# Feed-forward norms of two layers: rows are turned raw, the weight is multiplied in by feature columns, the root at the up evictions

## The reference, cut

```python
for layer in range(DEPTH):                       # DEPTH = 2
    h = rms_norm(x, g_mix[layer])
    qkv = h @ w_in[layer]
    ...
    x = x + mix @ w_out[layer]
    h2 = rms_norm(x, g_ffn[layer])               # the norm that the change touches
    x = x + conv_gated_mlp(h2, w_up[layer], conv_w[layer], conv_b[layer], w_down[layer])

def conv_gated_mlp(h, w_up, conv_w, conv_b, w_down):
    u = h @ w_up                                 # 1024 -> 2 x 2816
    u = causal convolution of width 3 along the tokens, per feature, + conv_b
    gate, val = jnp.split(u, 2, axis=-1)
    return (jax.nn.silu(gate) * val) @ w_down
```

## Time and profile before

| | |
|---|---|
| median of 3 runs | 1744.21 us |
| lowest, highest | 1742.28, 1744.73 us |
| the profiled execution, its own time | 1744.4 us |
| its span, first to last instruction | 1742.6 us |
| TensorE, VectorE, ScalarE, GpSimd busy | 97%, 66%, 47%, 41% of the span |
| mean granted TensorE clock | 0.996 |

### The profile page before, as it was taken

The page is one execution under the profiler, slowest core; times in us unless marked ns, Lnnn a source line. Parts: engine busy times, 40 slices in busy tenths (PEclk is TensorE's granted clock), DMA queues, the critical chain, the costliest instruction groups (busy, mean ns, idle before and its releaser), DMA issues.

```text
span 1742.6 us, 27224 instructions
## 1 busy us (share of the span) xinstructions
PE 1693.9 (97%) x10714; PEld 1456.7 (84%) x10714; DVE 1151.4 (66%) x2422; ACT 821.4 (47%) x1453; POOL 706.1 (41%) x384
## 2 busy tenths in 40 slices
PE   7999999999999998999999999999999999999997
PEld 6779998777799986544579999999999988888885
DVE  6755785756467585655332999999999644444443
ACT  5555655355476642122343554544444455555553
POOL 2424676133266811421163999700000144444443
PEclk9999999999999999999999999999999999999998
DMA  7333545463165463323353656544444466666664
GB/s 289 117 109 135 191 170 183 148 217 117 61 211 201 170 199 122 107 86 120 97 202 114 225 165 203 179 144 141 144 145 140 162 193 194 194 193 194 194 193 134
DMA packets 77456, 283.20 MB, mean 163 GB/s; under 512 B 8721, under 2 KB 8977, under 8 KB 77073
## 3 DMA queue, kind: packets, MB, share of 16 engines
q1 hardware_dynamic: 76032, 276.50, 48.5%
q10 hardware_dynamic: 1296, 4.97, 0.8%
HBM read 279.33 MB, written 2.10 MB: 161 GB/s over the span
## 4 chain that ended last, share of the span: by engine, by line
PE 79%; DVE 7%; POOL 4%; ACT 4%; issue 3%; DMA 1%; POOLq 0%; DVEq 0%; ACTq 0%
PE bank L542 63%; PE bank L533 8%; PE bank L597 5%; POOL wl L2117 4%; ACT wh L1112 2%; DVE att L1478 2%; PE bank L665 1%; DVE wl L1461 1%; ACT att L1115 1%; PE bank L967 1%; PE bank L889 1%; DVE ssb L1467 1%; DVE mix L1506 1%; DVE xs L1467 1%; PE bank L837 0%
## 5 line engine op out<-in xcount | busy, mean ns | idle before, releaser
L2117 POOL TENSOR_TENSOR wl<-raw,wh 128x1024 fp32r<-128x1024 f32 x213 | 547.6, 2582 | 696.5 <-ACT wh L1112 688.1
L542 PE MATMUL bank<-hh,wh 128*128 128x256 f32 x1856 | 526.5, 284 | 5.1 <-POOL wl L2117 4.2
L1112 ACT ACTIVATE wh<-raw 128x1024 fp32r<-128x1024 f32 x476 | 492.9, 1050 | 58.2 <-PE bank L542 39.4
L542 PE MATMUL bank<-hl,wh 128*128 128x256 f32 x1856 | 519.3, 280 | 0.0
L542 PE MATMUL bank<-hh,wl 128*128 128x256 f32 x1856 | 517.9, 279 | 0.0
L1461 DVE TENSOR_TENSOR wl<-raw,wh 128x1024 fp32r<-128x1024 f32 x263 | 353.8, 1351 | 93.8 <-ACT wh L1112 93.3
L542 PEld LDWEIGHTS bank<-hh,wh 128*128 128x128 f32 x1856 | 349.1, 188 | 6.6 <-POOL wl L2117 5.5
L542 PEld LDWEIGHTS bank<-hl,wh 128*128 128x128 f32 x1856 | 349.2, 188 | 0.0
L542 PEld LDWEIGHTS bank<-hh,wl 128*128 128x128 f32 x1856 | 349.0, 188 | 0.0
L1467 DVE TENSOR_TENSOR acl<-H,ach 128x256 fp32r<-128x256 f32 x128 | 87.6, 685 | 181.5 <-ACT ach L1115 181.5
L542 PE MATMUL bank<-wh,ach 128*128 128x512 f32 x512 | 199.2, 389 | 0.4 <-DVE acl L1467 0.4
(11 more groups left out here) (216 smaller groups left out, 2322.5 us busy)
## 6 DMA issues: line engine op xcount, KB each, us to landing
raw<-in_ut_dram SPq DMA_DIRECT2D x128, 512.0 KB, 3.5
raw<-in_vt_dram SPq DMA_DIRECT2D x128, 512.0 KB, 3.7
raw<-in_wup_dram SPq DMA_DIRECT2D x88, 512.0 KB, 4.1
raw<-in_win_dram SPq DMA_DIRECT2D x48, 512.0 KB, 4.6
raw<-in_wdown_dram SPq DMA_DIRECT2D x44, 512.0 KB, 4.2
raw<-in_wout_dram SPq DMA_DIRECT2D x24, 512.0 KB, 3.6
raw<-in_wga_dram SPq DMA_DIRECT2D x16, 512.0 KB, 3.6
raw<-in_wpq_dram SPq DMA_DIRECT2D x16, 512.0 KB, 4.7
```

Source lines behind the costliest of these rows:

```text
L542: m = p.e.matmul(out, lhs[i][a], rhs[i][b], start=start and i == 0 and j == 0, stop=stop and i == n - 1 and j == 2)
L1112: a.e.activation(high_of(u), raw_of(u), ACTF.Copy).then_inc(act_hi.up(("hi", u)), 1)
L2117: g.e.tensor_tensor(low_of(u), raw_of(u), high_of(u).bitcast(F32), ALU.subtract).then_inc(pool_lo.up(("lo", u)), 1)
```

## The change

The two feed-forward norms of the first block are taken apart.

- TensorE turns x itself, block by block, as soon as VectorE has added it (`x_turned`). The first block is turned ahead of the last quarter of the projection, and the dummy transposes of this place are gone.
- The weight is multiplied in when the turned blocks are split: ScalarE makes the high half of each block of 128 features with the feature's weight as its scale (`x_high`), and VectorE the low half with a multiply and a subtraction in one instruction (`x_low`). The weights come as 32 columns `gcol`, loaded once on ScalarE's queue. The two row units are no longer in `plan`, and no row is loaded or scaled.
- The root is found behind the splitting. VectorE spreads it to 128 columns per tile (`root_rows`), TensorE turns it after `f` = 0 of the up stage, and VectorE copies it out (`root_cols`). In each `f` VectorE then multiplies the bank of 128 x 512 in place by the root of each token, and the evictions wait for that (`upR`).
- In ScalarE's, VectorE's and GpSimd's lists, the splitting of the units of this place is moved against the norm's steps.
- Tensors move in SBUF: `hh` and `hl` are 2304 wide and the `f` stages start 16 elements in, `sta`, `con` and `sml` have other widths, and a scratch area is set to 1024.

```diff
-        hh, hl = scoped(sc_h, "hh", 2048, F32R), scoped(sc_h, "hl", 2048, F32R)
+        hh, hl = scoped(sc_h, "hh", 2304, F32R), scoped(sc_h, "hl", 2304, F32R)
...
-            stage(("row", "f", L), [(rows_d[2 + L], 1024, False)])
...
+        def hT_of(st):
+            o = 16 if st[0] == "f" else 0
+            return [w[:, o:o + 2048].rearrange("p (k t) -> p k t", k=8) for w in (hh, hl)]
...
+            def x_turned(st, t, k0, b, *after):
+                claim(b)
+                p.wait_ge(*after)
+                n = block_of(st, t, k0)[1]
+                for k in range(k0, k0 + n):
+                    m = p.e.transpose(banks[b][:, (k - k0) * 128:(k - k0) * 128 + 128], x[:, t, k * 128:(k + 1) * 128], ids[:, :])
...
@@ pe @@
-                for t in range(2):
-                    for j in (6, 7):
-                        out_unit(j, (t, ))
-                kept_streaming(8, 0)
-                for t, n in ((0, 22), (1, 6)):
-                    turned(("f", L), mix, 8, (t, ), lambda t, q: (dve_out, ("nrm", ("f", L), t, q)), of=(2, 3, 4, 5, 7))
-                    kept_streaming(n, 0)
+                st = ("f", L)
+                out_unit(6, (0, ))
+                out_unit(7, (0, ))
+                out_unit(6, (1, ))
+                free = ((0, 2, 3, 4, 7, 1), (0, 2, 5, 7, 6, 1))[L]
+                x_turned(st, 0, 0, free[0], dve_out, ("xa", L, 0, 0))
+                out_unit(7, (1, ))
+                x_turned(st, 1, 0, free[1], dve_out, ("xa", L, 1, 0))
+                x_turned(st, 1, 2, free[2], dve_out, ("xa", L, 1, 0))
+                x_turned(st, 0, 4, free[3], dve_out, ("xa", L, 0, 1))
+                x_turned(st, 1, 4, free[4], dve_out, ("xa", L, 1, 1))
+                x_turned(st, 1, 6, free[5], dve_out, ("xa", L, 1, 1))
                 for f in range(NTILE):
+                    if f == 1:
+                        p.wait_ge(dve_out, ("rb", st))
+                        for t in range(2):
+                            m = p.e.transpose(banks[b][:, tcols(t)], root_rows[:, tcols(t)], ids[:, :])
...
@@ act @@
+            def x_high(st, t, ks):
+                for k in ks:
+                    a.wait_ge(pe_out, ("T", st, t, block_of(st, t, k)[0]))
+                    do(hT_of(st)[0][:, k, tcols(t)], turned_block(st, t, k), ACTF.Identity, ("hTh", st, t, k), scale=gcol(st, k))
...
+                stream(first["wout", L] + 6)
+                x_high(st, 0, range(4))
                 half_squares(st, 0, mix, 0, dve_out, ev + (0, 0))
+                x_high(st, 1, range(4))
+                x_high(st, 0, range(4, 8))
+                x_high(st, 1, range(4, 8))
                 half_squares(st, 0, mix, 1, dve_out, ev + (0, 1))
-                stream(first["wout", L] + 6)
                 half_squares(st, 1, mix, 0, dve_out, ev + (1, 0))
                 half_squares(st, 1, mix, 1, dve_out, ev + (1, 1))
-                turned(st, (0,), 2)
                 stream(first["wout", L] + 7)
-                stream(first["row", "f", L])
-                turned(st, (1,), 2)
...
-                        a.wait_ge(pe_out, ("up", L, f, 1))
+                        a.wait_ge(dve_out, ("upR", L, f))
...
@@ dve @@
                 added(0, 0)
                 added(0, 1)
+                added(1, 0)
+                x_low(st, 0, range(4))
+                added(1, 1)
+                x_low(st, 1, range(4))
+                for k in range(4, 8):
+                    for t in range(2):
+                        x_low(st, t, (k, ))
                 stream(first["wout", L] + 6)
+                stream(first["wout", L] + 7)
                 mean(st, 0)
-                added(1, 0)
-                scale(st, 0, mix, row)
-                added(1, 1)
                 mean(st, 1)
-                turned(st, (0,), 1)
-                scale(st, 1, mix, row)
-                turned(st, (0,), 2, 1)
-                turned(st, (1,), 2)
-                stream(first["wout", L] + 7)
-                stream(row)
+                v.wait_ge(pool_out, ("rs", st, 0), ("rs", st, 1))
+                copy(root_rows.rearrange("p (a n) -> p a n", a=2), rstd[:, 0:2].unsqueeze(2).broadcast_to([128, 2, 128]), ("rb", st))
                 for f in range(NTILE):
                     stream(first["wup", L] + 2 * f)
                     stream(first["wup", L] + 2 * f + 1)
+                    if f == 0:
+                        v.wait_ge(pe_out, ("RT", st))
+                        copy(root_cols, ps("RT", st)[:, 0:256], ("R", st))
+                    both = ps("up", L, f)[:, :].rearrange("p (h t) -> p h t", h=2)
+                    v.wait_ge(pe_out, ("up", L, f, 1))
+                    tt(both, both, root_cols.unsqueeze(1).broadcast_to([128, 2, 256]), ALU.mult, ("upR", L, f))
...
@@ pool @@
+                stream(first["wout", L] + 6)
                 for t in range(2):
                     root(("f", L), t)
-                    g.wait_ge(dve_out, ("nrm", ("f", L), t, 1))
-                stream(first["wout", L] + 6)
                 stream(first["wout", L] + 7)
-                stream(first["row", "f", L])
...
-    nc = _bacc.Bacc("TRN2", target_bir_lowering=False, num_devices=1)
+    nc = _bacc.Bacc("TRN2", target_bir_lowering=False, num_devices=1, dynamic_dma_scratch_size=1024)
```

More of the change, by code:

```diff
@@ L114, in program @@
         early = ExitStack()
-        con_s = scoped(early, "con", K_W - 128)
-        sml_s = scoped(early, "sml", S_W)
+        con_s = scoped(early, "con", 1664)
+        sml_s = scoped(early, "sml", 896)
         tab_s = scoped(early, "tab", 8192)
@@ L303, in sml, with gcol, blocks, block_of @@
             return sml_s[:, c:c + n]
-        def hT(k, cols):
-            return hTh[:, k, cols], hTl[:, k, cols]
+        def hT_of(st):
+            o = 16 if st[0] == "f" else 0
+            return [w[:, o:o + 2048].rearrange("p (k t) -> p k t", k=8) for w in (hh, hl)]
+        def gcol(st, k):
+            return gcol_s[:, 8 * (st[1] + 2 * (st[0] == "f")) + k:8 * (st[1] + 2 * (st[0] == "f")) + k + 1]
+        def blocks(st, t):
+            return ((0, 2), (2, 2), (4, 2), (6, 2)) if st[0] == "f" and t else ((0, 4), (4, 4))
+        def block_of(st, t, k):
+            return [(k0, n) for k0, n in blocks(st, t) if k0 <= k < k0 + n][0]
+        def turned_block(st, t, k):
+            k0 = block_of(st, t, k)[0]
+            return ps("T", st, t, k0)[:, (k - k0) * 128:(k - k0) * 128 + 128]
+        def hT(st, k, cols):
+            return [w[:, k, cols] for w in hT_of(st)]
         iota = con(K_IOTA, 128)
@@ L334, in program @@
         tb = headtmp[:, 256:512].rearrange("p (h d) -> p h d", h=4)
+        root_rows, root_cols = headtmp[:, 0:256], headtmp[:, 256:512]
         NB = 4
@@ L590, in by_tokens @@
                         if plan[i][2]:
-                            m = mm3(banks[b][:, 0:cw], [hT(off + h * kper + k, tcols(t)) for k in range(kper)],
+                            m = mm3(banks[b][:, 0:cw], [hT(("n",), off + h * kper + k, tcols(t)) for k in range(kper)],
                                     [unit_pair(i, k, kper, slice(0, cw)) for k in range(kper)], h == 0, h == nu - 1,
@@ L616, in by_features @@
                             m = mm3(banks[b][:, 0:256], [unit_pair(i, k, kt, tcols(c)) for k in range(kt)],
-                                    [hT(off + k, ALLC) for k in range(kt)], True, True, ready)
+                                    [hT(("f", 2), off + k, ALLC) for k in range(kt)], True, True, ready)
                         else:
@@ L743, in out_unit @@
                             claim(b)
-                        m = mm3(banks[b][:, :], [hT(2 * h + k, tcols(t)) for k in range(2)], [unit_pair(i, k, 2, slice(0, 512)) for k in range(2)], h == 0, h == 3,
+                        m = mm3(banks[b][:, :], [hT(("n",), 2 * h + k, tcols(t)) for k in range(2)], [unit_pair(i, k, 2, slice(0, 512)) for k in range(2)], h == 0, h == 3,
                                 lambda k: p.wait_ge(dve_out, ("mT", L, h)))
@@ L798, in pe @@
                         m = mm3(banks[b][:, 256 * half:256 * half + 256], [unit_pair(i, k, 8, tcols(0)) for k in range(8)],
-                                [hT(k, ALLC) for k in range(8)], True, True, ready_both(("f", L)))
+                                [hT(("f", L), k, ALLC) for k in range(8)], True, True, ready_blocks(("f", L)))
                         m.then_inc(pe_out.up(("used", i), ("up", L, f, half)), 1)
@@ L1040, in hidden @@
                 claim(b)
-                m = mm3(banks[b][:, 0:256], [unit_pair(i, k, 8, tcols(0)) for k in range(8)], [hT(k, ALLC) for k in range(8)], True, True, ready_both(("f", 2)))
+                m = mm3(banks[b][:, 0:256], [unit_pair(i, k, 8, tcols(0)) for k in range(8)], [hT(("f", 2), k, ALLC) for k in range(8)], True, True, ready_both(("f", 2)))
                 m.then_inc(pe_out.up(("used", i), ("hid", j)), 1)
@@ L1159, in act @@
             load(ids[:, :], consts_d[:, 0:128], id_in, "id")
+            load(gcol_s[:, 0:32], gcol_d, g_in, "g")
```

(15 more changed lines are left out.)

43 lines of the change are left out of this document (27 added, 16 removed).

## The result

The changed kernel takes 1791.99 us (median, 1789.85 to 1795.29) beside 1743.24 us (1741.94 to 1744.73) for the kernel before on the same chip: ratio 1.028, 95% interval 1.0268 to 1.0292. It is 2.8% slower. The profiled execution took 1789.85 us with a span of 1788.0 us, 45.4 us more than the span of before; it is the fastest of the four, and by the medians the change costs 48.75 us. The forecast was 1793.5 us.

The account below looks back on a forecast made before the run. TensorE, busy 97%, was taken as the bound, with ScalarE's and VectorE's up-stage loop tying it without slack. Layer 0 20.4, layer 1 23.0 and slots 5.6 made 49.0 us on 1744.4: 1793.5 us, range 1765 to 1819.

Parts of the forecast that it names:

- The seam: Last output-projection matmul to first up matmul, 6.37 us: raw turns start sooner, f = 1 waits for the root; 0.9 us gained per layer.
- The loop: Up stage: multiply 0.69, eviction 0.55 and handovers add 1.3 us a period (1.0 to 2.0), 23.4 us a layer.
- The two sums: Delay until the sixth down unit in each layer: 20.4 us later in layer 0, 23.0 us later in layer 1.
- the new numbering: Up loop: the removed row unit shifts which periods are cheap, saving 2.6 us in layer 0 and 1.7 in layer 1.
- Slots: First expert units: key units move to slots 0 and 1, unit 0 starts 7.3 us late, 5.6 remain (bounds 3 and 8).
- Homes: Moved SBUF starts of the split halves of x: taken as 0, with 8 us either way as bound.
- the 49.0 of the sum: Total loss over the whole kernel: 20.4 + 23.0 + 5.6 us, added to the profiled execution's 1744.4 us.
- (a): Rival, up loop: TensorE stays the bound, multiply and eviction hidden, periods under 5.66 us; 1748 us, chance 0.08.
- (b): Rival, up loop at 5.66 us: each seam gives 2.0 us, slots cost nothing; 1740 us, at most 1732; chance 0.09.
- (c): Rival, up stages: starved TensorE falls to the half clock level, 5.65 becomes some 10.5 us; 1900 us, chance 0.03.
- the 80 to 85 that I named as a sign: Up windows: TensorE busy about 80 to 85 of 100 from the fifth f on, waiting for low halves of wup.
- (d): Rival, every matmul: moved SBUF starts change the pace by a per cent or more, 17 us; 1776 or 1811, chance 0.04.

Follow-up runs that it names:

- experiment 1: The changed kernel without the in-place multiply by the root, the first up eviction waiting for TensorE again: 1744.03 us, ratio 1.0004 to the kernel before.
- 2: The changed kernel with the same multiply placed ahead of that f's two low-half subtractions in VectorE's order: 1754.38 us, ratio 1.0076 to the kernel before.
- experiment 5: The changed kernel with early slots counted from 2 and the multiply in VectorE's pause from f = 4, before that ahead of the subtractions: 1738.74 us, ratio 0.9962.
- 7: The changed kernel with the multiply cut to 8 of the 256 columns of each half, at its old place behind the subtractions: 1773.75 us, ratio 1.0169.
- experiment 3: The changed kernel with early units' slots counted from 2, so the two key units lie in slots 2 and 3 again: 1785.01 us, ratio 1.0248.
- experiment 4: The kernel before with only the changed kernel's SBUF starts and widths, no instruction changed: 1740.38 us, ratio 0.9988.
- the fifth kernel: The kernel of experiment 5, with slots back and the multiply in VectorE's pause: 1738.74 us, ratio 0.9962.

## Why the prediction was right

**The seam.** The first up matmul was expected at 149.2 and came at 148.12; layer 0's second pair of splittings at 162.8 and 162.54. In layer 1 the pair starts 24.0 us behind the first addition to x instead of 19.9, 4.1 later; 3.75 was the forecast. `f` = 1 waits for the root, 1.0 us, and its first matmul starts at 155.7 instead of the 157.5 forecast. So the seam gives 1.9 us per layer and not 0.9: `f` = 2 starts 19.8 us behind the first addition to x in both layers, and 21.8 and 21.7 before. One term that was mis-sized is VectorE's 128-wide operation, 0.35 in the sum and 0.28 here:

```profile
147.57 1.39 DVE L1569 SCALAR_TENSOR_TENSOR hl<-bank,gcol,hh 128x128 fp32r<-128x128 f32 x5
```

This hardly moved the time, since the second pair of splittings, from which the loop runs, came about as forecast. VectorE's timeline there (layer 0), the copy of the root's rows, two subtractions, the copy of its columns and the first multiply:

```profile
155.16 0.29 DVE L1535 COPY headtmp<-sta 128x256 f32<-128x256 f32 x1 [1.06 <-POOL sta L2188]
156.06 2.72 DVE L1513 TENSOR_TENSOR wl<-raw,wh 128x1024 fp32r<-128x1024 f32 x1 [0.61 <-ACT wh L1156]
158.71 0.41 DVE L1535 COPY headtmp<-bank 128x256 f32<-128x256 f32 x1
159.15 0.70 DVE L1519 TENSOR_TENSOR bank<-bank,headtmp 128x512 f32<-128x512 f32 x1
```

**The loop.** This is the step that carried the forecast, and it held: 1.33 us a period against 1.3, 20.98 us for three against 20.9, and the mechanism is shown by experiments 1, 2, 5 and 7. From the second to the twentieth pair both layers take 23.7 us more than in experiment 1 (124.5 instead of 100.8, and 124.6 instead of 100.9); 23.4 were forecast. The multiply took 0.683 to 0.700 us in all 44 executions. The Trainium skill, page "SBUF — State Buffer", section "Who interferes with whom", says that a VectorE instruction with at most one SBUF input, outside the two-port modes, does not contend with GpSimd. The multiply has one, and the trace agrees: the multiply at 612.07 took 0.69 inside GpSimd's subtraction of 611.02 to 614.35. The rows of experiment 2 agree from the other side: the subtraction, with two, was stretched to 3.38.

**The two sums.** Layer 0's sixth down unit was ready at 311.50 (309.11 + 2.39) instead of 293.02: 18.5 later, 20.4 forecast. Layer 1 cost 24.1, of which 23.0 were forecast. In layer 0 the twentieth pair came at 287.03, not 289.5, and the sixth down unit followed it by 24.5 us (23.9 forecast). The term that was off is the new numbering: without the multiply (experiment 1) the stretch from the second to the twentieth pair takes 100.8 us instead of 105.9, 5.1 less, where 2.6 had been put down. In layer 1 the second pair, that stretch and the tail each came 0.4 to 0.6 us later than forecast.

**Slots.** 5.6 forecast, 7.0 by the times of experiment 3, 7.4 by the trace. The mechanism (unit 0 takes over the times of unit 2, 7.3 late) is what the row shows, 7.14. The step that was off is that later units would give 1.7 of it back: that much was lost again to the clock, at 0.96 in the 52 us behind the pause, where experiment 3 has 1.00. The 24 matmuls of unit 0 took 4.87 us instead of 2.82.

**Homes.** This was the wrong step: 0 was taken, with the words that nothing in the trace says that an address matters. -4.5 was measured in the trace of experiment 4. Of two kernels that differ in 64 bytes one is 9.2 us faster; the 8 us of the bound were about the right size.

**The number.** Against the 49.0 of the sum the trace has 1.2 less for layer 0, 1.1 more for layer 1, 1.8 more at the key units and 5.1 less elsewhere, which experiment 4 puts mostly down to the homes: 45.6 at the first expert matmul. The mechanism carried the forecast, but that the median lies only 1.5 us from it is in part luck: terms that were mis-sized or left out cancel in part, and the profiled execution, from which the parts are read, is 2.1 us below the median.

**The rivals.** (a) and (b) asked for 5.66 us periods. The multiply's place forbids them; in the fifth kernel, with another place, periods are as (b) wants them and the time is 1738.74, near its 1740; but (b) has no gain from the homes in it, so that the number agrees by luck. The 0.63 at the start, which (c) puts down to the half level, was read from the pace, a matmul each 0.43 us and later each 0.23; the profile grants 1.00 there. (c), the clock, did appear, but hidden. Here are windows of the changed kernel in the up stages; before, both were at 1.00 with TensorE busy all the time. It is busy for 87 or 88% now, a little above the 80 to 85 that I named as a sign.

```profile
220.00:260.00 40.00, 35.03 (x270) 0.91 0.46 147
530.00:580.00 50.00, 43.53 (x339) 0.93 0.46 158
```

The clock fell to its half level (1.2 GHz) for a part of these stretches, in which TensorE had paused up to 3.8 us at a time:

```profile
226.00:228.00 2.00, 2.00 (x11) 0.50 0.96 387
```

The Trainium skill, page "TensorE: Matmul & The Clock Gate", section "HAM oscillation — how this bites in real kernels", tells of a kernel in which a wait for data between bursts of matmuls brings the slow level each time; here it came for a small part, and cost nothing visible in the up stages, since ScalarE's and VectorE's loop set the pace there (20.98 for three, with the clock down or not). It cost at the first expert units. (d) came true in small, as above, on the fast side.

## What to carry to other kernels

When two engines run in fixed order and hand work to each other, an operation's price is its place: in layer 1 the same 0.69 us multiply cost 1.33 us a period behind the subtractions, nothing under a splitting, and nothing in a pause of 0.94 us. In layer 0, under a splitting, it changed the order of two subtractions that hinder each other and cost 12 us. Before adding an operation to such a loop, look in the timeline for a pause of that engine that is long enough, and put it there. And count what else is moved with it: units that change their number change their slots (7 us here), and a tensor's start is a parameter worth trying once (9 us here).

## What the runs showed of the hardware

- The pace of matmuls depends on where their moving operand starts in SBUF: an expert up unit took 3.703 to 3.770 us, at full clock and equal traffic, for shifts of 32 and 128 bytes. 32 and 64 bytes were fast, 0 and 128 slow; no other shifts were tried. A shift of 64 bytes in some stages moved 1747.93 to 1738.74.
- Of two subtractions of 128x1024 that overlap on VectorE and GpSimd, the one that starts second pays: VectorE 3.38 instead of 1.64 when it was 0.11 us behind, GpSimd 3.39 instead of 2.40 when VectorE was ahead. VectorE's takes 1.22 at its shortest.
- A VectorE multiply that reads and writes the same 128x512 of PSUM takes 0.69, as an addition of that shape that writes SBUF does (0.685); a 128x16 one takes 0.17.
- In the up and down stages TensorE paused ten times for more than 2 us (2.22 to 3.85). Around six of these pauses the clock was at the half level for 3 to 4 us: after the 3.85 us that ended at 203.06 matmuls came 0.12 us apart, then 0.21 from 204.5 to 207.8, then 0.12 again. The other four, one of 3.60 us among them (ended at 530.51), left it at 1.00. After one of 7.14 us matmuls came 0.21 apart from the second on, for some 4 us; after 1.28 us in the kernel before they came 0.12 apart. Over 40 and 50 us of the up stages the grant was 0.91 and 0.93.
